# Copies of the transposed probabilities in the latent attention shared by ScalarE and VectorE, four tiles each

## The reference

```python
kv = (_rmsnorm(c_kv, g) @ w_kv_b).reshape(b, s, 8, 128 + 128)
k_nope, v = kv[..., :128], kv[..., 128:]
def block(args):                      # a block of 128 queries, all 8 heads
    qn, qp = args
    sc = (einsum('bqhd,bkhd->bhqk', qn, k_nope) + einsum('bqhr,bkr->bhqk', qp, k_pe)) * scale
    p = softmax(sc, axis=-1)          # 128 queries x 1024 keys for each head
    return einsum('bhqk,bkhd->bqhd', p, v)
o = o * silu(z)
```

## The kernel before

| q | PE | DVE, after `dve_probs(q)` and `dve_max(q+1)` |
|---|---|---|
| 0 | scores 1, values product of the head before, transposes 0, V0 | mod_out and gate of the head before, 3 products |
| 1 | scores 2, V1, transposes 1, (R0) | rope in even heads, (R0), 3 products |
| 2 | scores 3, values product 0, transposes 2, (R1) | (R1), 2 products |
| 3 | scores 4, Q0, transposes 3, mod_pe 0 | Q0 low, rope in odd heads |
| 4 | scores 5, values product 1, transposes 4, Q1 | mod_out 0, gate 0, Q1 low, 2 products |
| 5 | scores 6, K0, transposes 5, K1 | K0 low, K1 low, 4 products |
| 6 | scores 7, values product 2, transposes 6 | 2 products |
| 7 | scores 0 of the next head, mod_pe 1, transposes 7 | none |

## Time and profile before

### The profile page before, as it was taken

The page is one execution under the profiler, slowest core; times in us unless marked ns, Lnnn a source line. Parts: engine busy times, 40 slices in busy tenths (PEclk is TensorE's granted clock), DMA queues, the critical chain, the costliest instruction groups (busy, mean ns, idle before and its releaser), DMA issues.

```text
span 3080.3 us, 34996 instructions
## 1 busy us (share of the span) xinstructions
PE 2777.5 (90%) x13113; PEld 2176.5 (71%) x13113; DVE 1675.0 (54%) x2177; ACT 1307.7 (42%) x1842; POOL 0.2 (0%) x4
## 2 busy tenths in 40 slices
PE   4899999997889988898987789998689999999996
PEld 2677777775667766676766567666567878888775
DVE  5688888887453055555554635554644434334344
ACT  4567666665224133333332435565424313223232
POOL 0000000000000000000000000000000000000000
PEclk7999999998889999999999889999799999999998
DMA  7211111110211111121221310000211111111111
GB/s 257 98 39 43 48 48 44 45 34 27 89 34 45 50 56 47 50 67 49 67 61 41 106 41 21 28 15 14 82 41 41 44 51 46 50 48 40 49 42 68
DMA packets 215821, 166.96 MB, mean 54 GB/s; under 512 B 9562, under 2 KB 203058, under 8 KB 215730
## 3 DMA queue, kind: packets, MB, share of 16 engines
q1 hardware_dynamic: 215530, 165.68, 17.3%
q10 hardware_dynamic: 200, 0.06, 0.0%
HBM read 153.14 MB, written 12.58 MB: 54 GB/s over the span
## 4 chain that ended last, share of the span: by engine, by line
PE 79%; DVE 8%; ACT 5%; DVEq 2%; issue 2%; SPq 1%; DMA 1%; ACTq 0%
PE PS L516 19%; PE PS L518 18%; PE PS L517 18%; PE PS L1012 4%; PE PS L1666 3%; PE PS L985 2%; PE PS L999 2%; PE PS L989 1%; PE PS L1621 1%; PE PS L1656 1%; PE PS L2155 1%; PE PS L2168 1%; DVEq L1808 1%; PE PS L2179 1%; DVE rest L507 1%
## 5 line engine op out<-in xcount | busy, mean ns | idle before, releaser
L516 PE MATMUL PS<-h_high,w_high 128*128 128x512 f32 x2144 | 858.8, 401 | 59.8 <-DVE h_low L583 18.9
L517 PE MATMUL PS<-h_low,w_high 128*128 128x512 f32 x2144 | 844.7, 394 | 0.0
L518 PE MATMUL PS<-h_high,w_low 128*128 128x512 f32 x2144 | 844.6, 394 | 0.0
L516 PEld LDWEIGHTS PS<-h_high,w_high 128*128 128x128 f32 x2144 | 408.7, 191 | 159.6 <-issue 62.7
L518 PEld LDWEIGHTS PS<-h_high,w_low 128*128 128x128 f32 x2144 | 407.7, 190 | 87.1
L517 PEld LDWEIGHTS PS<-h_low,w_high 128*128 128x128 f32 x2144 | 408.8, 191 | 81.8 <-issue 0.5
L538 DVE TENSOR_TENSOR w_low<-raw_weights,w_high 128x1024 fp32r<-128x1024 f32 (+2 forms) x159 | 182.9, 1155 | 216.3 <-ACT w_high L533 215.5
L533 ACT ACTIVATE w_high<-raw_weights 128x1024 fp32r<-128x1024 f32 (+2 forms) x159 | 158.6, 1001 | 243.8 <-PE PS L518 233.1
L765 DVE SCALAR_TENSOR_TENSOR residual<-PS,rest,residual 128x512 f32 (+1 forms) x112 | 83.3, 750 | 244.2 <-PE PS L518 240.5
L1088 ACT ACTIVATE residual<-PS,rest 128x1024 f32<-128x1024 f32 x128 | 141.4, 1110 | 174.3 <-DVE rest L1217 174.3
L2717 DVE SCALAR_TENSOR_TENSOR gated<-rest,gated 128x1024 f32<-128x1024 f32 x44 | 56.6, 1286 | 255.0 <-ACT gated L2686 255.0
(11 more groups left out here) (307 smaller groups left out, 3972.5 us busy)
## 6 DMA issues: line engine op xcount, KB each, us to landing
raw_weights<-in_w_in SPq DMA_DIRECT2D x59, 512.0 KB, 4.1
activations<-in_w_ada SPq DMA_DIRECT2D x16, 1536.0 KB, 7.0
raw_weights<-in_w_up SPq DMA_DIRECT2D x44, 512.0 KB, 3.9
raw_weights<-in_w_out SPq DMA_DIRECT2D x24, 512.0 KB, 4.1
rest<-in_ada_w SPq DMA_DIRECT2D x16, 576.0 KB, 4.9
activations<-in_ada_w SPq DMA_DIRECT2D x8, 1024.0 KB, 13.7
x_kept<-residual SPq DMA_DIRECT2D x2, 4096.0 KB, 13.3
residual<-x_kept SPq DMA_DIRECT2D x2, 4096.0 KB, 13.5
```

The costliest lines, as they stand in the source:

```text
L516: e.matmul(out_, wh[:, k, :], xh[:, k, cols], start=first, stop=False)
L517: e.matmul(out_, wh[:, k, :], xl[:, k, cols], start=False, stop=False)
L518: return e.matmul(out_, wl[:, k, :], xh[:, k, cols], start=False, stop=last_k)
```

## The change

Two banks of transposes are copied by two engines. ACT now copies bank 6 (tiles 4 to 7), DVE bank 5 (tiles 0 to 3), with a new semaphore `ted`. The next transposes and the values product wait for both. In DVE's order the new copy stands behind `dve_probs(q)`, `dve_max(q+1)` and the set of `BEFORE`, and ahead of mod_out, the gate, the rope, the set of `AFTER` and the modulation's products. The set of `BEFORE` moves ahead of mod_out and gate; no tile q has both.

```diff
@@ pe_trans, pe_pv
             wait(e, te, 8 * t.h + q)
+            wait(e, ted, 8 * t.h + q)
...
             e.wait_ge(te, 8 * t.h + (2 * m + 2))
+            e.wait_ge(ted, 8 * t.h + (2 * m + 2))
@@ act_evac
-            e.activation(PT[:, :, (q % 2) * P:(q % 2 + 1) * P], banks(5, 2).rearrange("p (a b) -> p a b", a=NT),
+            e.activation(PT[:, 4:8, (q % 2) * P:(q % 2 + 1) * P], banks(6).rearrange("p (a b) -> p a b", a=4),
                          ACT.Copy).then_inc(te, 1)
@@
+        def dve_evac(e, t, q):
+            e.wait_ge(tr, 8 * t.h + (q + 1))
+            e.tensor_copy(PT[:, 0:4, (q % 2) * P:(q % 2 + 1) * P],
+                          banks(5).rearrange("p (a b) -> p a b", a=4)).then_inc(ted, 1)
@@ dve_head
                 elif more:
                     dve_max(e, t.next(), 0)
+                if wanted(t, BEFORE.get(q), more):
+                    dve_set(e, t, BEFORE[q])
+                dve_evac(e, t, q)
                 if q == 0 and prev is not None:
                     dve_mod_out(e, prev, 1)
                     dve_gate(e, prev, 1)
                 if q == 4:
                     dve_mod_out(e, t, 0)
                     dve_gate(e, t, 0)
-                if wanted(t, BEFORE.get(q), more):
-                    dve_set(e, t, BEFORE[q])
```

More of the change, by code:

```diff
@@ L1536, in latent_attention @@
         sc, mx, ex, pr = sem("la_scores"), sem("la_max"), sem("la_exp"), sem("la_probs")
-        tr, te = sem("la_tr"), sem("la_tr_out")
+        tr, te, ted = sem("la_tr"), sem("la_tr_out"), sem("la_tr_out_dve")
         pv, gt = sem("la_pv"), sem("la_gated")
```

## The result

| | before | after |
|---|---|---|
| time, median | 3082.51 us (4 runs, 3076.97 to 3085.21) | 3113.39 us (4 runs, 3101.35 to 3117.84) |
| ratio, 95% interval | | 1.0091 (1.007 to 1.0113) |
| profiled execution | 3082.07 us, span 3080.3 | 3101.35 us, span 3099.5 |
| latent attention, first V0 to the end of the last gate | 482.67 us | 508.23 us |

The kernel became slower by 28 us (22 to 35). A second comparison of the same changed kernel gave 1.0097 (1.0082 to 1.0113). The stages behind it took 1503 us before and after.

The account below looks back on a forecast made before the run. PE was taken to bound the kernel, waiting nearly only for DVE. The terms 7.4 + 7.4 - 1.7 + 2.4 + 1.4 + 3.2 = 20.1 us gave 3102.2 or 3105.2, taken as 3104, range 3095 to 3114.

Parts of the forecast that it names:

- (a): V0 in heads 1 to 7 waits for mod_out, now behind DVE's copy: 7 x 1.05 = 7.4 us longer.
- (b): Q1 in heads 0 to 6 waits for mod_out, now behind DVE's copy: 7.4 us longer.
- (c): Transposes 2 in four even heads come 0.43 us earlier through ACT's shorter copy of transposes 1: -1.7 us.
- (d): Tile 2 of even heads: DVE's copy delays the low part of Q0, so mod_pe 0 waits longer: 4 x 0.61 = 2.4 us.
- (e): Tiles 6 and 7: copy and products delay transposes 7 by about 0.2 us in each of 7 heads: 1.4 us.
- (f): The last head, without Q and K sets: DVE's copies delay tiles 3, 4 and 6: 3.2 us, bounds 1.5 and 4.5.
- a rival with 12 us and a chance of 0.11: New idle stretches bring PE 8 more spells at half clock, 1.5 us each: 12 us more, 3116; chance 0.11.
- The rival of delays made up: PE's later waits swallow the delays at V0 and Q1, leaving about 5 us: 3090; chance 0.06.
- that of the shorter copy: Each tile's copy ends 0.33 us earlier and PE's 2.2 us of waits for it go: 3.9 us less, 3081; chance 0.03.

Follow-up runs that it names:

- experiment 1: The changed kernel with mod_out and gate ahead of VectorE's copy, all 64 tiles still shared; ratio 1.0024 to the kernel before, +7.4 us.
- 2: The changed kernel with only tiles 0 and 4 of each head shared, ScalarE copying the other six whole; ratio 1.0073 to the kernel before, +22 us.
- 6: The changed kernel with only tile 0 of each head shared, ScalarE copying the other seven whole; ratio 1.0043 to the kernel before, +13 us.
- experiment 4: The kernel before, with VectorE waiting for the transposes at the new copy's place and copying one unused column instead; ratio 1.0042, +13 us.
- experiment 8: Changed kernel sharing only even heads' tile 1 and the last head's tiles 5, 6, 7; mod_out and gate first, tile 6's copy behind products; 1.0017, +5 us.

## Why the prediction was right

Its time of 3104 was 9 us low against the median, by its sum 20 us of the 28; the range 3095 to 3114 held the median of 3113.4 by 0.6 us, which at that margin is luck: one spell more would have put it outside. The signs that it gave are there: V0 and Q1 idle and released by L823, mod_pe 0 at 1.22 us, transposes 2 at 0.65, K1 unchanged, odd heads of 71.2 us and even ones of 60.3 where no spell lies in them, the stages behind the same. Step by step, against the stage's 25.6 us. (a) and (b) are measured from the start of the transposes to the start of the scores behind V0 or Q1, the others likewise between starts:

| step | forecast | measured |
|---|---|---|
| (a) V0, heads 1 to 7 | 7.4 | 3 x 1.12, 3 x 1.19 and 1.13: 8.1 |
| (b) Q1, heads 0 to 6 | 7.4 | 7 x 1.12 = 7.8 |
| (c) transposes 2, even heads | -1.7 | 4 x (0.65 - 1.08) = -1.7 |
| (d) mod_pe 0, even heads | +2.4 | 4 x 0.6 = 2.4 |
| (e) tiles 6 and 7 | +1.4 | transposes 7 start 0.35 later, the next head's start makes up 0.13: 7 x 0.22 = 1.5 |
| (f) last head | +3.2 | 3.3 up to transposes 7, 0.2 less of waiting behind them: 3.0 |
| slow spells, heads 0 to 6 | 0 (in a rival) | three even heads at 1.6, less 1.6 in head 0 before: 3.1 |
| slow spell, last head | 0 | twice as long as before: 1.4 |

(a) and (b) are shown by experiment 1, which takes them away alone, and by 2 and 6, which keep them alone; that nothing behind them makes them up, by K1's wait, unchanged to 0.02 us. The rival of delays made up is dead, and so is that of the shorter copy: the waits that it counts on did go, and were worth what (c) says and a little in the last head. The reason given for the size of a wait was half right: I added up copy and mod_out, while experiment 4 shows that in heads 1 to 6 the copy in part hides issue time that would be there without it. The sum came out because the two run side by side. What it left out are the 0.1 us that the first products lose behind the wait.

The term that was mis-sized is the clock's. I had put it into a rival with 12 us and a chance of 0.11, in place of a term of the forecast. It came in part: 4.5 us of the 25.6. The price was right, 1.6 us for a spell against my 1.5, and the place was not: no spell begins at the new waits ahead of V0 and Q1. The kernel before has spells too, but of its three in heads 0 to 6 the two in odd heads cost nothing, because PE waits for VectorE behind them anyway (68.8 us with and without one); those in the odd heads of the changed kernel lie in the same place and cost nothing either (71.2 us each). The three new ones in even heads lie in dense work of PE.

What brings a spell is open in part. In heads 0 to 6 the fourteen profiles have 81 of them, and each begins at a long wait of PE, between 0.4 us before its end and 2.1 us behind it: 32 at K1's (2.25 us), 27 at Q0's in odd heads (2.34), 8 at mod_pe 0's in odd heads where it is 2.33, and 14 at mod_pe 0's in even heads where it is 1.22. None begins at V0 or Q1 (0.3 to 0.93 us), none at transposes 2 (0.64 to 1.8 us), none at mod_pe 0 where it waits 0.6 to 0.8, and none at a filled wait. So the change made a new place for spells by step (d), not by (a) and (b). Which of these waits gets one isn't settled: about half get none, and edits elsewhere shift the choice. Nor is it settled why the medians differ by 28 to 31 us and the stage by 25.6 to 27.2; that is within the interval. The stage's start alone, behind the same instructions, lay between 1086.6 and 1097.5 us in the fourteen profiles.

## What to carry to other kernels

Before an engine gets new work, look at what stands behind the place where it goes in, and which semaphore there is waited for by the engine that bounds the kernel. Here the new instruction's own length was the small part; that it waits for something late, and holds a short instruction that was early, was the large one, 11.3 of 15.9 us. And take work from an engine only where the chain goes through it: ScalarE gave up 27 us of 64 copies, of which 1.7 lay on the path in the even heads, and less than that in the last one.

## What the runs showed of the hardware

An instruction of VectorE whose addresses are computed in registers started 0.33 us behind the start of one of 0.15 us, the same with fixed addresses 0.07 us behind it, and either of them 0.61 us behind the start of a copy of 0.69 us (experiment 4 and the changed kernel). Its register arithmetic, 0.10 and 0.04 us, runs beside a long predecessor, and is bare behind a short one.

A wait of PE of 0.85 us cost 1.12: the overlap with the transposes ahead of it, 0.16 us, and 0.1 us in the first products came on top.

And small shifts of timing move PE's spells at half clock, some 3 us each, from one long wait to another. One cost between nothing, where PE waits again soon behind it, and 1.65 us; one of twice the length 3.2 us (head 5 of experiment 4, 73.6 us against 70.4). In a kernel whose heads repeat, the same place can be hit in each of them, and the gain of 1.7 us in the even heads of experiment 8 was more than eaten by three spells at 1.6 us.
